# Splitting the odd stage's weights on GpSimd in whole instructions of 1,024 columns instead of four of 256

## The chip, the core and the metric

The kernel runs on one core of a Trainium2 chip. Its engines are TensorE (PE in the rows, with its weight loads as PEld), VectorE (DVE), ScalarE (ACT), GpSimd (POOL) and SyncE (SP), which issues most of the DMAs. The metric is the device time of one execution in microseconds; three runs of the kernel before gave 3427.5, 3423.56 and 3424.99 us, median 3424.99. Numbers such as 1036.13 are times from the span's start in the profiled execution.

## The reference

Two small transformer-like blocks run one after the other on 512 latent tokens and 256 context tokens of width 1,024. The first block has an even layer (a chunk MLP beside differential attention), then an odd layer (windowed attention with a sink), each followed by a SwiGLU network; the second block has a gated recurrent layer and a latent attention layer. The change lies in the projections of the odd layer, `h @ w_qkv`:

```python
q, k, v = jnp.split(h @ w_qkv, [C_Q_WIDTH, C_Q_WIDTH + C_KV_WIDTH], axis=-1)
q = apply_rope(q.reshape(b, s_len, C_HEADS, HEAD_DIM), cos, sin)...
k = apply_rope(k.reshape(b, s_len, C_KV_HEADS, HEAD_DIM), cos, sin)
kc, vc = jnp.split(hc @ w_qkv[:, C_Q_WIDTH:], 2, axis=-1)
...
s = einsum(q, k) * ATTN_SCALE                     # a band of up to 384 keys, and 256 context keys
p = softmax(concatenate(scores + [s_sink]))       # per 128 queries and head
out = einsum(p, v)
```

The weights `w_qkv` are 12 tiles of 128x1024 in float32: 8 for the queries, 2 for the keys, 2 for the values.

## The kernel before, in words

**Products in three parts.** A product of float32 matrices is made of three float32r matmuls: high weights by high tokens, high weights by low tokens, low weights by high tokens. So each weight tile must be split into a high part (rounded to float32r) and a low part (the tile minus its high part). In the odd stage GpSimd does that, in `split` (lines 661 to 670). Line 665 multiplies a piece of the tile in `ringA` by one and writes it rounded to `ringB_r`; a drain follows (line 666); line 668 subtracts and writes the low part into `ringA_r`, in place; then the semaphore `splitA` rises. The argument `n` says how many columns one instruction takes.

**The ring.** `ringA` has four slots. SP loads a tile (line 509) when `readA` says that TensorE has done with what was in the slot, and GpSimd splits it when `landedA` says that it has landed. All twelve tiles of the stage go through this in order, tile by tile (`split_A`, lines 672 to 677). The stages before and after use the same function: `ffn_out0` splits in whole tiles, `odd_out` in quarters, `ffn_in1` and `ffn_out1` whole.

**The odd stage.** First VectorE and ScalarE make the normalised tokens: line 2665 scales them, ScalarE's line 1972 rounds the high part, line 2587 makes the low part `a_r`; before that, line 2649 makes the coefficients. TensorE then computes tiles 0, 1 and 2 together, chunk by chunk (line 812), and tile 3 in two halves (line 1340). VectorE turns the first queries and keys by the rotary tables (lines 3049, 3050 and 3052, each with 512 columns, the two sets one after the other). The attention follows in 32 units, U = 0 to 31. For each, TensorE makes scores (1421 to 1430), VectorE the row maxima (3059 to 3064), ScalarE the exponentials (2237), VectorE the sums and the normalised p (3070 to 3074), TensorE the transposes (1444), ScalarE copies (2245), and TensorE the product with the values (1455). Between these TensorE puts pieces of the projections of tiles 4 to 11 (line 1340). Scores of the first unit wait for both rotary steps; scores of a later unit wait for the exponentials of the one before. Each engine works through its instructions in the written order; semaphores alone join them.

**Which tiles when.** Tiles 4 to 7 are loaded as slots 0 to 3 come free, near the end of the products of tiles 0 to 3. Tiles 8 to 11 are loaded one at a time, each when TensorE has finished the projection of the tile four places before it.

Of the kernel before, what the change touches and what calls it, by code (L numbers as in the profile page):

```python
# [15 lines left out]
D = 1024  # L16
# [88 lines left out]
def build(nc, streamA, streamB, streamC, x_in, ctx2_in, smalls_in, consts_in, lvl_in, sgu_in, out):  # L105
    with ExitStack() as ctx:
# [5 lines left out]
        def sem(name):  # L112
            if name not in sems:
                sems[name] = ctx.enter_context(nc.semaphore(name))
            return sems[name]

        def both(name, shape):

            with nc.sbuf_tensor(name, shape, F32) as v:
                pass  # L120
            return v, sb(name + "_r", shape, F32R)
# [9 lines left out]
        ringA, ringA_r = both("ringA", [P, RA, D])  # L131
        ringB, ringB_r = both("ringB", [P, RB, D])
# [85 lines left out]
        def landedA_at(name, g, k):  # L218
            return 16 * ((START_A[name] + k) // RA + 1) + g * (16 * COUNT[name][1] // RA)
# [177 lines left out]
        def high_slot(name, s):  # L397

            return (s + 1) % RA if name == "mla_out" else s
# [259 lines left out]
        def _(pool):  # L659

            def split(ring, ring_r, slot, high_r, high_slot, done, n=D // 4):

                parts = [slice(at, at + n) for at in range(0, D, n)]
                for t in parts:
                    nc.gpsimd.tensor_tensor(high_r[:, high_slot, t], ring[:, slot, t], ones[:, 0:1].broadcast_to([P, n]), ALU.mult)  # L665
                pool.drain()  # L666
                for t in parts:
                    last = nc.gpsimd.tensor_tensor(ring_r[:, slot, t], ring[:, slot, t], high_r[:, high_slot, t].bitcast(F32),  # L668
                                                   ALU.subtract)
                last.then_inc(sem(done), 1)  # L670

            def split_A(name):
                with pool.Fori(0, COUNT[name][0]) as g:
                    for k in range(COUNT[name][1]):
                        s = k % RA
                        pool.wait_ge(landedA[s], landedA_at(name, g, k))
                        split(ringA, ringA_r, s, ringB_r, high_slot(name, s), "splitA", D // 4 if name in ("even_out", "odd") else D)

            def split_hg_out():

# [92 lines left out]
            split_B("even")  # L773
            pool.wait_ge(sem("ev_exp"), 48)
            split_A("even_out")
            wi_products()
            for g in range(COUNT["ffn_out0"][0]):
                for k in range(COUNT["ffn_out0"][1]):
                    pool.wait_ge(landedA[k % RA], landedA_at("ffn_out0", g, k))
                    if g == 0 and k < RA:  # L780
                        pool.wait_ge(sem("wi_read"), max(n for n in range(len(PRODUCTS)) if n % RB == k) + 1)
                    split(ringA, ringA_r, k % RA, ringB_r, k % RA, "splitA", D)
            split_A("odd")
            pool.wait_ge(sem("od_p"), 60)
            split_odd_out()
            split_A("ffn_in1")
            split_A("ffn_out1")
            pool.wait_ge(sem("hg_free"), HEADS + 1)
# [2815 lines left out]
```

## Time and profile before

| what | value |
|---|---|
| runs | 3427.5, 3423.56, 3424.99 us |
| profiled execution | 3423.45 us, its span 3421.7 us |
| TensorE busy | 3251.4 us (95%) |
| VectorE busy | 2040.7 us (60%) |
| ScalarE busy | 1259.1 us (37%) |
| GpSimd busy | 1117.8 us (33%), 909 instructions |
| GpSimd in the odd stage, line 665 | 48 instructions of 128x256, 29.7 us |
| GpSimd in the odd stage, line 668 | 48 instructions of 128x256, 37.7 us |

The span is what the profiler saw on the core; the execution's own time is 1.75 us longer. A busy engine is not the same as one that others wait for: the waits in square brackets behind a row say how long its engine had sat idle before it, and what ended that.

### The profile page before, as it was taken

To read this page: it belongs to the slowest core of one execution; us is meant where nothing else is said; L and a number is where in the kernel's file an instruction comes from. 1 tells how busy PE (TensorE), PEld (TensorE's weight loads), DVE (VectorE), ACT (ScalarE), POOL (GpSimd) and SP (SyncE) were. 2 spreads that over 40 slices of the span, in tenths; PEclk is the share of its full clock that TensorE was granted. 3 is DMA by queue.
4 is the path that set the end of the run, shared out by engine and by line. 5 is a ranking of instruction groups with operands and counts; after the bars stand their busy time and mean duration, and the time that the engine had idled before them with its cause. 6 is when DMAs were issued, how large, how long until landed. Compare 5 with 4: busy or idle time off the path is not lost.

```text
span 3421.7 us, 53881 instructions
## 1 busy us (share of the span) xinstructions
PE 3251.4 (95%) x21096; PEld 2864.3 (84%) x21096; DVE 2040.7 (60%) x3136; ACT 1259.1 (37%) x2098; POOL 1117.8 (33%) x909
## 2 busy tenths in 40 slices
PE   7998989999998988999999999999999998999998
PEld 5776889999986666777799999999999697788876
DVE  4455554445345654023758787887878764566667
ACT  3444253332224541101244334343443223455542
POOL 3341565556544136677800000000000161222225
PEclk9999999999999999999999999999999997999999
DMA  6222244434211124444321111111110321111112
GB/s 265 87 87 111 86 172 150 162 125 181 81 56 38 32 75 166 169 176 166 106 77 53 53 49 52 49 49 44 44 45 31 117 62 62 38 49 37 48 68 80
DMA packets 85626, 307.62 MB, mean 90 GB/s; under 512 B 8496, under 2 KB 10544, under 8 KB 84400
## 3 DMA queue, kind: packets, MB, share of 16 engines
q1 hardware_dynamic: 78688, 286.89, 25.1%
q10 hardware_dynamic: 6736, 17.83, 1.4%
q8 instruction: 153, 2.51, 0.3%
q14 instruction: 49, 0.40, 0.0%
HBM read 281.61 MB, written 23.07 MB: 89 GB/s over the span
## 4 chain that ended last, share of the span: by engine, by line
PE 71%; DVE 14%; DVEq 4%; issue 4%; POOL 3%; ACT 3%; POOLq 1%; DMA 1%; SPq 0%; ACTq 0%
PE ps L812 20%; PE ps L951 14%; PE ps L1107 9%; PE ps L1691 4%; PE ps L1729 2%; DVE arena L3136 2%; DVEq L3127 2%; DVE arena L3126 2%; DVE rstd L3142 2%; PE ps L927 2%; DVE arena L3132 1%; PE ps L1340 1%; POOL ringA_r L668 1%; DVE arena L3123 1%; POOLq L666 1%
## 5 line engine op out<-in xcount | busy, mean ns | idle before, releaser
L665 POOL TENSOR_TENSOR ringB_r<-ringA,consts 128x1024 fp32r<-128x1024 f32 (+1 forms) x226 | 318.5, 1423 | 1545.6 <-DVE arena L3211 1021.5
L812 PE MATMUL ps<-x_r,ringA_r 128*128 128x384 f32 (+1 forms) x1912 | 557.0, 356 | 8.7 <-DVE a_r L2587 5.3
L812 PE MATMUL ps<-x_r,ringB_r 128*128 128x384 f32 (+1 forms) x1912 | 543.2, 349 | 10.1 <-DVE a_r L2587 9.0
L668 POOL TENSOR_TENSOR ringA_r<-ringA,ringB_r 128x1024 fp32r<-128x1024 f32 (+1 forms) x226 | 392.9, 1753 | 21.3 <-issue 0.4
L812 PEld LDWEIGHTS ps<-x_r,ringB_r 128*128 128x128 f32 x1912 | 350.1, 189 | 34.0 <-POOL ringA_r L668 9.2
L812 PE MATMUL ps<-a_r,ringA_r 128*128 128x384 f32 x1472 | 375.3, 335 | 0.0
L812 PEld LDWEIGHTS ps<-x_r,ringA_r 128*128 128x128 f32 x1912 | 338.7, 189 | 35.8 <-issue 8.5
L951 PE MATMUL ps<-a_r,ringB_r 128*128 128x384 f32 (+1 forms) x1376 | 340.4, 357 | 20.5 <-DVE a_r L2699 11.6
L951 PEld LDWEIGHTS ps<-a_r,ringB_r 128*128 128x128 f32 x1376 | 251.1, 191 | 41.3 <-DVE a_r L2699 17.7
L2699 DVE TENSOR_TENSOR a_r<-arena,a_r 128x768 fp32r<-128x768 f32 (+1 forms) x120 | 176.0, 1504 | 169.7 <-ACT a_r L2133 169.4
L812 PEld LDWEIGHTS ps<-a_r,ringA_r 128*128 128x128 f32 x1472 | 266.7, 188 | 0.0
L951 PE MATMUL ps<-a_r,ringA_r 128*128 128x384 f32 (+1 forms) x688 | 205.5, 355 | 0.0
L1107 PE MATMUL ps<-arena_r,ringB_r 128*128 128x384 f32 x1008 | 189.7, 339 | 2.1 <-POOL ringB_r L744 1.4
L2133 ACT ACTIVATE a_r<-arena 128x768 fp32r<-128x768 f32 (+1 forms) x120 | 83.3, 733 | 278.4 <-PE ps L951 270.4
L1107 PEld LDWEIGHTS ps<-arena_r,ringB_r 128*128 128x128 f32 x1008 | 176.8, 190 | 2.8 <-POOL ringB_r L744 1.7
L812 PE MATMUL ps<-a_r,ringB_r 128*128 128x512 f32 (+1 forms) x440 | 164.2, 385 | 0.0
L716 POOL TENSOR_TENSOR x_r<-ringA,consts 128x256 fp32r<-128x256 f32 x64 | 37.2, 613 | 342.9 <-DVE arena_r L3284 283.9
L744 POOL TENSOR_TENSOR ringB_r<-ringB,ringB_r 128x512 fp32r<-128x512 f32 x84 | 110.0, 1321 | 117.0 <-DVE ringB L2784 82.8
L2910 DVE TENSOR_TENSOR arena<-arena,ps 128x512 f32<-128x512 f32 x22 | 15.1, 688 | 218.6 <-PE ps L812 207.1
L1691 PE MATMUL ps<-arena_r 128*128 128x256 f32 (+1 forms) x768 | 141.8, 310 | 2.3 <-DVE arena_r L3270 1.5
L2699 DVE TENSOR_TENSOR arena_r<-arena,arena_r 128x768 fp32r<-128x768 f32 (+1 forms) x64 | 110.5, 1765 | 49.7 <-ACT arena_r L2133 49.4
L1107 PE MATMUL ps<-x_r,ringB_r 128*128 128x384 f32 x504 | 139.9, 338 | 0.0
(427 smaller groups left out, 6747.2 us busy)
## 6 DMA issues: line engine op xcount, KB each, us to landing
ringA<-streamA SPq DMA_DIRECT2D x232, 512.0 KB, 3.6
arena<-streamC SPq DMA_DIRECT2D x140, 512.0 KB, 6.5
ringB<-streamB SPq DMA_DIRECT2D x100, 512.0 KB, 3.6
x_scratch<-x ACTq DMA_DIRECT2D x8, 1024.0 KB, 6.8
x<-x_in SPq DMA_DIRECT2D x2, 3072.0 KB, 11.1
hid_scratch<-arena SPq DMA_DIRECT2D x16, 384.0 KB, 3.9
arena<-hid_scratch SPq DMA_DIRECT2D x1, 6144.0 KB, 22.4
x<-x_scratch SPq DMA_DIRECT2D x3, 2048.0 KB, 11.0
```

Of the source, the lines that this page charges most:

```text
L665: nc.gpsimd.tensor_tensor(high_r[:, high_slot, t], ring[:, slot, t], ones[:, 0:1].broadcast_to([P, n]), ALU.mult)
L668: last = nc.gpsimd.tensor_tensor(ring_r[:, slot, t], ring[:, slot, t], high_r[:, high_slot, t].bitcast(F32), ALU.subtract)
L744: nc.gpsimd.tensor_tensor(low, weight_source(p, j), high.bitcast(F32), ALU.subtract).then_inc(sem("wi_low"), 1)
L812: mm = nc.tensor.matmul(ps[:, bank + half, 0:tn], wk, src[:, k, t], start=k == 0 and i == 0, stop=k == DC - 1 and i == 2)
L927: mm = nc.tensor.matmul(ps[32 * j:32 * j + 32, b, at:at + 256], spad[:, vec, 2 * t + k, :], ring[:, t, k, r * 256:(r + 1) * 256], start=t ...
L951: mm = nc.tensor.matmul(ps[:, 2 * n + half, 0:tn], w, src[:, t], start=k == 0 and i == 0, stop=k == nk - 1 and i == 2)
L1107: mm = nc.tensor.matmul(ps[:, bank, 0:HALF], wk[:, w], src, start=p in ("P1", "P2", "P5", "P3") and c == 0 and i == 0, stop=c == 3 and i = ...
L1691: mm = nc.tensor.matmul(out, w, src, start=start and i == 0, stop=stop and i == 2, skip_group_check=True)
L1729: mm = nc.tensor.matmul(ps[:, 7, :], w, src[:, k, 0:LAT], start=k == 0 and i == 0, stop=k == DC - 1 and i == 2)
L2133: nc.scalar.activation(out_ring(name, p, chunk.shape[-1])[0], chunk, ACT.Copy).then_inc(sem("out_high"), 1)
L2699: TT(low, chunk, high.bitcast(F32), ALU.subtract).then_inc(sem("out_low"), 1)
L3126: TT(halves(H["ql"][:, p, :], h), halves(B["q"], h), P_queries, ALU.mult).then_inc(sem("hg_lvl"), 1)
```

## The change

In the odd stage the last argument of `split` becomes `D` (1,024) instead of `D // 4` (256), so that a tile takes one instruction of line 665 and one of line 668 instead of four of each. The stage `even_out` keeps its quarters, and so does `odd_out`, which has its own loop. Nothing else is changed: not the order of tiles, the loads, nor what any engine waits for.

```diff
                     for k in range(COUNT[name][1]):
                         s = k % RA
                         pool.wait_ge(landedA[s], landedA_at(name, g, k))
-                        split(ringA, ringA_r, s, ringB_r, high_slot(name, s), "splitA", D // 4 if name in ("even_out", "odd") else D)
+                        split(ringA, ringA_r, s, ringB_r, high_slot(name, s), "splitA", D // 4 if name == "even_out" else D)
```

On GpSimd, from the last tiles of `ffn_out0` into the first three of the odd stage's twelve, there stands before (`ringA` is the tile that was loaded, `ringB_r` its high part, `ringA_r` its low part, `consts` holds the ones):

```order
143 L665 TENSOR_TENSOR ringB_r<-ringA,consts 128x1024
144 L668 TENSOR_TENSOR ringA_r<-ringA,ringB_r 128x1024
145 L673 UNCONDITIONAL_BRANCH
146 L665 TENSOR_TENSOR ringB_r<-ringA,consts 128x256 x4
147 L668 TENSOR_TENSOR ringA_r<-ringA,ringB_r 128x256 x4
148 L665 TENSOR_TENSOR ringB_r<-ringA,consts 128x256 x4
149 L668 TENSOR_TENSOR ringA_r<-ringA,ringB_r 128x256 x4
150 L665 TENSOR_TENSOR ringB_r<-ringA,consts 128x256 x4
151 L668 TENSOR_TENSOR ringA_r<-ringA,ringB_r 128x256 x4
```

And at the same place now:

```order
143 L665 TENSOR_TENSOR ringB_r<-ringA,consts 128x1024
144 L668 TENSOR_TENSOR ringA_r<-ringA,ringB_r 128x1024
145 L673 UNCONDITIONAL_BRANCH
146 L665 TENSOR_TENSOR ringB_r<-ringA,consts 128x1024
147 L668 TENSOR_TENSOR ringA_r<-ringA,ringB_r 128x1024
148 L665 TENSOR_TENSOR ringB_r<-ringA,consts 128x1024
149 L668 TENSOR_TENSOR ringA_r<-ringA,ringB_r 128x1024
150 L665 TENSOR_TENSOR ringB_r<-ringA,consts 128x1024
151 L668 TENSOR_TENSOR ringA_r<-ringA,ringB_r 128x1024
```

No instruction has moved. Each group of four has become one, so the stage has 24 of these instructions where it had 96. The order of every other engine is the same.

## Rows read from the trace of the kernel before

**Rows 1.** The page: the chain that ended last, by engine.

```profile
PE 71%; DVE 14%; DVEq 4%; issue 4%; POOL 3%; ACT 3%; POOLq 1%; DMA 1%; SPq 0%; ACTq 0%
```

**Rows 2.** Timeline of GpSimd, 964 to 988: start, duration, what, [idle before <-releaser].

```profile
964.95 1.89 POOL L665 TENSOR_TENSOR ringB_r<-ringA,consts 128x1024 fp32r<-128x1024 f32 x1 [4.51 <-DMA ringA<-streamA]
966.99 2.38 POOL L668 TENSOR_TENSOR ringA_r<-ringA,ringB_r 128x1024 fp32r<-128x1024 f32 x1
...
981.06 2.33 POOL L665 TENSOR_TENSOR ringB_r<-ringA,consts 128x256 fp32r<-128x256 f32 x4 [2.90 <-DMA ringA<-streamA]
983.53 2.82 POOL L668 TENSOR_TENSOR ringA_r<-ringA,ringB_r 128x256 fp32r<-128x256 f32 x4
```

**Rows 3.** Timeline of GpSimd, tiles 2 and 3 of the odd stage.

```profile
995.85 2.75 POOL L665 TENSOR_TENSOR ringB_r<-ringA,consts 128x256 fp32r<-128x256 f32 x4 [9.50 <-DMA ringA<-streamA]
...
1003.93 3.22 POOL L668 TENSOR_TENSOR ringA_r<-ringA,ringB_r 128x256 fp32r<-128x256 f32 x4
```

**Rows 4.** Timeline of VectorE, the low parts of the first normalised tokens.

```profile
1005.61 1.82 DVE L2587 SCALAR_TENSOR_TENSOR a_r<-a,mod,x_r 128x512 fp32r<-128x512 f32 x2 [0.20 <-ACT x_r L1972]
...
1008.41 1.14 DVE L2587 SCALAR_TENSOR_TENSOR a_r<-a,mod,x_r 128x512 fp32r<-128x512 f32 x2
```

**Rows 5.** Timeline of GpSimd, tiles 4 to 7.

```profile
1033.58 2.33 POOL L665 TENSOR_TENSOR ringB_r<-ringA,consts 128x256 fp32r<-128x256 f32 x4 [26.43 <-DMA ringA<-streamA]
1036.05 4.22 POOL L668 TENSOR_TENSOR ringA_r<-ringA,ringB_r 128x256 fp32r<-128x256 f32 x4
1040.23 2.77 POOL L665 TENSOR_TENSOR ringB_r<-ringA,consts 128x256 fp32r<-128x256 f32 x4
...
1053.90 2.81 POOL L668 TENSOR_TENSOR ringA_r<-ringA,ringB_r 128x256 fp32r<-128x256 f32 x4
```

**Rows 6.** Timeline of VectorE beside tiles 4 to 6.

```profile
1036.13 1.20 DVE L3050 TENSOR_TENSOR arena<-arena,consts 128x512 f32<-128x512 f32 x1
1037.41 1.07 DVE L3052 TENSOR_TENSOR arena<-arena 128x512 f32<-128x512 f32 x1
...
1039.01 0.68 DVE L3050 TENSOR_TENSOR arena<-arena,consts 128x512 f32<-128x512 f32 x1
1039.76 1.06 DVE L3052 TENSOR_TENSOR arena<-arena 128x512 f32<-128x512 f32 x1
1042.35 1.29 DVE L3059 TENSOR_REDUCE st<-ps 128x1 f32<-128x512 f32 x2 [1.53 <-PE ps L1430]
...
1043.96 0.61 DVE L3063 TENSOR_SCALAR st<-st 128x2 f32<-128x2 f32 x1
1044.48 0.15 DVE L3064 TENSOR_TENSOR st<-smalls,st 128x2 f32<-128x2 f32 x1
```

**Rows 7.** Timeline of TensorE, the first scores.

```profile
1040.96 0.70 PE L1421 MATMUL ps<-arena 64*128 64x256 f32 x4 [1.18 <-DVE arena L3052]
```

**Rows 8.** Timeline of GpSimd, whole instructions in ffn_in1 and ffn_out1.

```profile
1306.65 2.35 POOL L668 TENSOR_TENSOR ringA_r<-ringA,ringB_r 128x1024 fp32r<-128x1024 f32 x1
...
1591.95 2.34 POOL L665 TENSOR_TENSOR ringB_r<-ringA,consts 128x1024 fp32r<-128x1024 f32 x1
```

**Rows 9.** Timeline of VectorE beside these.

```profile
1307.12 1.90 DVE L2649 SCALAR_TENSOR_TENSOR coef<-mod,smalls 128x16 f32<-128x16 f32 x1
...
1586.53 13.40 DVE L2699 TENSOR_TENSOR a_r<-arena,a_r 128x512 fp32r<-128x512 f32 x6 [3.11 <-ACT a_r L2133]
```

**Rows 10.** Timeline of VectorE beside tile 8.

```profile
1064.96 1.01 DVE L3074 TENSOR_SCALAR arena<-arena,st 128x640 f32<-128x640 f32 x1
...
1067.74 0.73 DVE L3064 TENSOR_TENSOR st<-smalls,st 128x2 f32<-128x2 f32 x1
```

**Rows 11.** Windows: length, each engine's busy us, then granted clock, DMA share, GB/s.

```profile
1046.00:1051.00 5.00, 4.74 (x19) 2.98 (x19) 3.44 (x8) 0.80 (x3) 4.86 (x8) 0.50 0.00 0
...
1071.00:1076.00 5.00, 3.11 (x34) 2.04 (x30) 3.56 (x12) 2.19 (x6) 0.43 (x1) 1.00 0.00 0
...
1131.00:1136.00 5.00, 5.00 (x33) 3.84 (x32) 3.31 (x9) 1.52 (x5) 3.89 (x7) 1.00 0.06 21
```

## The prediction

> **What bounds the kernel now.** I read the page first: TensorE holds 71% of the chain that ended last, VectorE 14%, GpSimd 3% [rows 1]. GpSimd is no bound over the whole, so the question is what its instructions do to others in the odd stage. Next came GpSimd's timeline there, then VectorE's in the same stretches, and last the TensorE windows.
>
> The reader is to see three things. GpSimd waits for the DMA of its tile, not the other way: 9.50 us before tile 2, 26.43 us before tile 4 [rows 3, 5]. Tiles 4 to 7 then form one burst without an idle bracket, from 1033.58 to 1056.71 [rows 5]. And in that burst VectorE does the rotary products and the first maxima, with TensorE waiting: the first scores at 1040.96 waited 1.18 us for VectorE's L3052 [rows 7]. The weights are not late there; VectorE is.
>
> **The change: what it saves.** A tile cost 2.33 us for L665 and 2.82 for L668 where VectorE kept away, and 5.29 us from first start to last end (981.06 to 986.35). Whole instructions of the stage before cost 1.89 and 2.38, and 4.42 us in all (964.95 to 969.37) [rows 2]. So 0.87 us less a tile, 12 tiles: 10.4 us of GpSimd time, over 72 fewer instructions. It is worth something only where a reader waits. TensorE starts on tiles 0 to 2 when the first normalised tokens are there, at 1007.43 (1005.61 + 1.82), and tile 3's L668 is already at work from 1003.93 [rows 3, 4]. Tile 4's split ended at 1040.27 [rows 5]; in TensorE's order its products stand behind the scores of two units, and the second scores wait for exponentials later than 1044.6 [rows 6]. I cost the saving itself at nothing; what hides it is that earlier work of TensorE.
>
> The shorter splits do one thing for the norm. Tile 2's split starts at 995.85 [rows 3]. With the old collision kept (2.75 against 2.33, so 0.42), whole it is 2.31 + 0.14 + 2.38, to 1000.7; tile 3 then runs to about 1005.1, where before its L668 ran 1003.93 to 1007.15. VectorE's first two L2587, which TensorE waits for, start at 1005.61 and took 1.82 us; the next two took 1.14 [rows 3, 4]. Tile 3 would be out of their way: **-0.7 us**.
>
> **The change: what it costs.** The trace shows what a VectorE instruction does that meets a whole GpSimd instruction. At 1306.65 GpSimd's L668 ran 2.35 us, to 1309.00; VectorE's L2649, all of 128x16, began at 1307.12 and took 1.90, to 1309.02 [rows 8, 9]. It waited for the end of the whole instruction. In a burst like ours both alternate: six L2699 took 13.40 us, 2.23 each, and GpSimd's L665 there 2.34, 0.45 over its 1.89 [rows 2, 8, 9]. So the one that waits gets its turn next, and VectorE gets one such operation per GpSimd instruction. (The Trainium skill, SBUF — State Buffer, "Who interferes with whom", says that whoever issues first has the shared port pair for the whole instruction, and that a tensor_tensor with two inputs in SBUF and a fast tensor_scalar contend while tensor_reduce does not; the trace agrees with the 1.90.) Which operations of ours are touched is seen from the stretched ones: L3050 1.20 and L3052 1.07 and 1.06 against 0.68 for the L3050 that met nothing, L3063 0.61 for two columns; the reductions L3059 from PSUM are not [rows 6]. With quarters such a wait ends after at most 0.8 us; whole it lasts up to 1.9 or 2.4.
>
> I walk the burst on the old clock, with 1.89 for L665, 2.35 for L668, and 0.55 for a 512-column VectorE operation once it has the turn. Tile 4: L665 1033.58 to 1035.47, L668 1035.61 to 1037.99. VectorE's first L3050 wants to start at 1036.13: it runs 1037.99 to 1038.55. Tile 5's L665 stood in line and takes 1038.55 to 1040.42; the first L3052 ends at 1040.97. L668 of tile 5 to 1043.3; second L3050 to 1043.85; L665 of tile 6 to 1045.7; second L3052 ends at 1046.25. Before it ended at 1040.82 [rows 6]: **+5.4 us** on the scores, which wait for nothing else. Scores and the reductions take as long as before (1.5 + 1.3 us and a little), so that L3061 wants its turn at 1049.1, while L665 of tile 7 holds to 1050.5. L3063 then waits for tile 7's L668, to 1053.0, and L3064 ends at 1053.3. Before, from the end of L3052 to the end of L3064 it was 1040.82 to 1044.63, 3.8 us [rows 6]; now 7.0: **+3.2 us**. The exponentials wait for it, and the second scores for them. GpSimd is then done, and what follows in VectorE is free. The bounds of these 8.6 us: below, if a waiting operation got in among the 1,024 columns, nothing is added and the stretches of the old rows go (0.52 + 0.38 + 0.37 + 0.44 = -1.7); above, TensorE's clock. It idles longer, and after a window like this the granted clock was 0.50, the 1.2 GHz level [rows 11]. I take no more of it than before, since the slow stretch moves along with the idle one; it may cost 1.5 us more.
>
> Queued behind each waiting VectorE instruction is its whole stream of maxima and normalisations; ScalarE's exponentials and TensorE's scores and transposes wait for these, and SP's next loads for TensorE's release of a slot. All of it moves along, so the later splits meet the same VectorE work as before.
>
> Tiles 8 to 11 are split singly, at 1065.00 and three times more. Tile 8: L3074 began at 1064.96 and took 1.01, about half of it waiting, so GpSimd had the turn [rows 10]; whole, L3074 ends at 1067.4 (+1.4). L668 then runs 1067.4 to 1069.75; L3061 wants 1068.7 and waits; L3064 ends at 1070.3 instead of 1068.47 (+1.8). The rotary step behind it is then free of GpSimd and regains some; the p that the transposes wait for comes +1.0 later, and TensorE idles there already (busy 3.11 of 5.00 us) [rows 11]. Tile 9 falls on the same work, with L3061 at the very edge: +0.8. Tiles 10 and 11 fall where TensorE is busy with projection pieces (5.00 of 5.00 us at tile 11 [rows 11]): 0.1 and 0, and at most 1.0 and 1.7 if that cover fails. Together **+1.9 us**, between -1.8 (no such lock; the waiting inside the 1.01 and the 0.73 of rows 10, about 1.0 a tile in tiles 8 and 9, less what lay off the path) and +6.3.
>
> Tiles 0 and 1 meet only VectorE work that reads PSUM. The sum: -0.7 + 5.4 + 3.2 + 1.9 = **+9.8 us**. The profiled execution took 3423.45 us (span 3421.7), so 3433.3; the median shown, 3424.99, lies 1.5 above it, and by that it would be 3434.8. I say **3434 us**.
>
> **The rivals.** (a) *The waits are there but partly absorbed.* If VectorE slips into the 0.14 us between L665 and L668 or at a changed phase, or part of the wait lies beside TensorE's leftover pieces, half of the 8.6 goes and the single tiles cost 0 to 1: +3 to +5, 3427 to 3429. For it: in the old rows some operations (the second L3050, 0.68) met no wait at all. Against it: the burst has GpSimd always standing in line, the scores already waited 1.18 us, and the sum of the waits is fixed by when the burst ends, near 1053.
>
> (b) *No lock: the port is shared in small pieces, so longer instructions stretch VectorE no more than quarters did, or less.* Then -0.7 - 1.7 - 1.8 = -4.2, 3419 against the profiled execution, 3421 against the median: within what can't be told from no change. Against it stands the 1.90 us for 16 columns.
>
> (c) *The other side: GpSimd's time is the bound.* If TensorE or the port waited for every split, all 10.4 us would come back: 3413 to 3415, faster. It decides from the point where a tile's first product starts within 0.9 us of the end of its split. For it: TensorE's start after 1007.43 lies right behind L668's end at 1007.15. Against it: that L668 is tile 3's, whose products come after all of tiles 0 to 2; everywhere else POOL is the one that waits for the DMA. [...]
>
> (d) *More than I walked.* The clock and the cover at tiles 10 and 11 fail: +9.8 + 1.5 + 2.6, 3437 to 3439.
>
> **How the numbers follow.** Less than about 0.2% of 3425, 6.9 us, is what a measurement of this kernel can't tell from no change. My forecast with (d): 0.79, nearly all above 3431.9. (a): 0.14. (b): 0.05. (c): 0.02. The range leaves out (b), (c) and a little above: 3427 to 3440. Faster 0.02, same 0.20, slower 0.78.
>
> **What would show it.** In the profile after: L665 and L668 of the stage as 12 rows each of 128x1024, tiles 4 to 7 done about 3 us earlier after their start; the first scores (L1421) waiting some 6 us for L3052 instead of 1.18; L3050, L3052, L3061 or L3063 of 1.5 to 2.6 us in the burst, one per GpSimd instruction; the start of L812 0.7 us earlier; the first split of odd_out some 10 us later. I am wrong if the L3052 before the first scores ends before 1043, if no VectorE operation of the stage exceeds 1.3 us (b), or if the delay at 1053 has vanished by the stage's end (a).

## The result, and the profile after

| | before | after |
|---|---|---|
| median, us (range, runs) | 3425.34 (3423.56 to 3428.97, 8) | 3435.81 (3432.02 to 3441.31, 8) |
| ratio after / before | | 1.0031, 95% interval 1.0022 to 1.0041 |
| profiled execution, its span | 3423.45, 3421.7 | 3436.25, 3434.5 |
| VectorE busy | 2040.7 | 2051.9 |
| GpSimd busy, instructions | 1117.8, 909 | 1106.7, 837 |

The kernel became slower by 10.5 us (7.5 to 14 by the interval); 3434 was predicted, in 3427 to 3440. GpSimd saved 11.1 us and VectorE's busy time grew by 11.2 with the same instructions: one that waits for GpSimd counts as busy (L3063, 2.36 us below, took 0.61 before). The shares of the chain that ended last [rows 1] moved little, TensorE's from 71% to 68% and GpSimd's from 3% to 4%:

```profile
PE 68%; DVE 14%; issue 4%; DVEq 4%; POOL 4%; ACT 3%; POOLq 2%; DMA 1%; SPq 0%; ACTq 0%
```

GpSimd's timeline after, tiles 4 to 7 (start, duration, instruction), answers to [rows 5]:

```profile
1035.98 1.89 POOL L665 TENSOR_TENSOR ringB_r<-ringA,consts 128x1024 fp32r<-128x1024 f32 x1 [28.21 <-DMA ringA<-streamA]
1038.02 2.40 POOL L668 TENSOR_TENSOR ringA_r<-ringA,ringB_r 128x1024 fp32r<-128x1024 f32 x1
1040.37 2.34 POOL L665 TENSOR_TENSOR ringB_r<-ringA,consts 128x1024 fp32r<-128x1024 f32 x1
1042.86 2.60 POOL L668 TENSOR_TENSOR ringA_r<-ringA,ringB_r 128x1024 fp32r<-128x1024 f32 x1
1045.43 2.34 POOL L665 TENSOR_TENSOR ringB_r<-ringA,consts 128x1024 fp32r<-128x1024 f32 x1
...
1050.47 1.89 POOL L665 TENSOR_TENSOR ringB_r<-ringA,consts 128x1024 fp32r<-128x1024 f32 x1
1052.51 2.34 POOL L668 TENSOR_TENSOR ringA_r<-ringA,ringB_r 128x1024 fp32r<-128x1024 f32 x1
```

And VectorE's beside it, to set against [rows 6]:

```profile
1037.93 0.69 DVE L3049 TENSOR_TENSOR arena<-ps,consts 128x512 f32<-128x512 f32 x1 [14.06 <-PE ps L1325]
1038.53 2.43 DVE L3050 TENSOR_TENSOR arena<-arena,consts 128x512 f32<-128x512 f32 x1
1041.04 2.23 DVE L3052 TENSOR_TENSOR arena<-arena 128x512 f32<-128x512 f32 x1
...
1043.79 2.23 DVE L3050 TENSOR_TENSOR arena<-arena,consts 128x512 f32<-128x512 f32 x1
1046.09 2.22 DVE L3052 TENSOR_TENSOR arena<-arena 128x512 f32<-128x512 f32 x1
1050.90 1.29 DVE L3059 TENSOR_REDUCE st<-ps 128x1 f32<-128x512 f32 x2 [2.59 <-PE ps L1430]
1052.27 0.16 DVE L3061 SCALAR_TENSOR_TENSOR st<-st,smalls 128x2 f32<-128x2 f32 x1
1052.51 2.36 DVE L3063 TENSOR_SCALAR st<-st 128x2 f32<-128x2 f32 x1
1054.78 0.15 DVE L3064 TENSOR_TENSOR st<-smalls,st 128x2 f32<-128x2 f32 x1
```

Read the two side by side. The burst lasts 18.87 us (1035.98 to 1054.85) where it lasted 23.13. But L3050 starts at 1038.53 inside GpSimd's L668, which ends at 1040.42, and ends at 1040.96, about 0.55 us later. Each of the four rotary operations with both inputs in SBUF ends about 0.55 us after the end of a GpSimd instruction: one gets through per instruction of 1,024 columns. Two columns wait as long as 512: L3063 takes 2.36 us and ends with the burst. L3049 (0.69) and L3059 (1.29), which read PSUM, wait for nothing.

TensorE's first scores, to set against [rows 7]:

```profile
1048.46 1.23 PE L1421 MATMUL ps<-arena 64*128 64x256 f32 x4 [6.28 <-DVE arena L3052]
```

They waited 6.28 us instead of 1.18, and then took 1.23 us instead of 0.70. The second is the clock. Windows of the kernel after (length; PE, PEld, DVE, ACT, POOL busy; then granted clock, DMA share, GB/s), and of the kernel before at the same times:

```profile
1045.00:1050.00 5.00, 1.54 (x8) 1.27 (x8) 3.23 (x2) 0.00 (x0) 4.86 (x3) 0.50 0.00 0
1050.00:1055.00 5.00, 0.86 (x6) 0.13 (x2) 3.87 (x5) 0.03 (x1) 4.70 (x3) 0.50 0.00 0
1055.00:1060.00 5.00, 3.44 (x15) 2.20 (x16) 1.89 (x7) 1.50 (x5) 0.00 (x0) 0.50 0.00 0
```

```profile
1045.00:1050.00 5.00, 3.74 (x17) 2.50 (x18) 2.88 (x7) 1.20 (x4) 4.86 (x8) 0.53 0.00 0
1050.00:1055.00 5.00, 5.00 (x19) 3.38 (x19) 1.98 (x5) 0.98 (x2) 4.86 (x9) 0.78 0.01 3
1055.00:1060.00 5.00, 5.00 (x43) 3.62 (x42) 3.51 (x9) 2.24 (x8) 1.71 (x3) 1.00 0.00 0
```

In both kernels TensorE idles and then runs at the 1.2 GHz level. After, it idles longer, and windows of 1 us from 1036 to 1096 give 17 us at the low level instead of 7 (a window counts in full at a granted clock of 0.50, not at all at 1.00, and in proportion between).

**The stage in parts.** To compare kernels whose starts differ by some us, I cut each trace at events of the stage:

| part, us | before | after | difference |
|---|---|---|---|
| last residual step of ffn_out0 (VectorE L2717) to TensorE's first L812 | 13.48 | 12.80 | -0.68 |
| to the first L3049 | 27.95 | 28.26 | +0.31 |
| rotary step, to the end of the second L3052 | 5.29 | 10.38 | +5.09 |
| first maxima, to the end of the first L3064 | 3.81 | 6.62 | +2.81 |
| to the first split of odd_out | 195.51 | 195.86 | +0.35 |
| whole stage | 246.04 | 253.92 | +7.9 |

"Stage" means this whole below. What lies before it (994.1 and 996.87 from the span's start) and behind it (2181.56 and 2183.71) is the same code, and over the other eight kernels of this case it varies from 992.0 to 996.2 and from 2179.8 to 2187.7. So 4.9 us of the 12.8 between the two spans lie outside the stage; I take them for scatter, though the change's own 996.87 is the latest start of all ten. Inside the stage, parts in which two kernels do the same work agree closely: the rotary step took 4.02 or 4.03 us in the three kernels with a wait and in the one without reading, and 10.35 and 10.38 in the two with a whole burst. A profile thus tells the stage more sharply than the total, though each stage below is of one profile.

### The profile page after: what moved, and what is told of

It is laid out like the page before. It is cut to its first block, busy times and chain, and to the rows that moved or that the text cites. A ratio compares the mean times of both kernels' runs of the same rounds, so it can differ in the third digit from the quotient of the medians.

```text
span 3434.5 us, 53809 instructions
## 1 busy us (share of the span) xinstructions
PE 3251.8 (95%) x21096; PEld 2864.8 (83%) x21096; DVE 2051.9 (60%) x3136; ACT 1259.2 (37%) x2098; POOL 1106.7 (32%) x837
## 4 chain that ended last, share of the span: by engine, by line
PE 68%; DVE 14%; issue 4%; DVEq 4%; POOL 4%; ACT 3%; POOLq 2%; DMA 1%; SPq 0%; ACTq 0%
PE ps L812 19%; PE ps L951 13%; PE ps L1107 9%; PE ps L1691 4%; PE ps L1729 2%; DVE arena L3136 2%; POOL ringA_r L668 2%; DVEq L3127 2%; POOLq L666 2%; DVE arena L3126 2%; DVE rstd L3142 2%; DVE arena L3132 1%; PE ps L1340 1%; DVE arena L3123 1%; PE ps L927 1%
## 5 line engine op out<-in xcount | busy, mean ns | idle before, releaser
L665 POOL TENSOR_TENSOR ringB_r<-ringA,consts 128x1024 fp32r<-128x1024 f32 (+1 forms) x190 | 312.8, 1655 | 1566.7 <-DVE arena L3211 1021.7
L812 PE MATMUL ps<-x_r,ringA_r 128*128 128x384 f32 (+1 forms) x1912 | 558.0, 357 | 11.1 <-DVE a_r L2587 4.7
L812 PE MATMUL ps<-x_r,ringB_r 128*128 128x384 f32 (+1 forms) x1912 | 544.8, 350 | 10.5 <-DVE a_r L2587 8.4
L668 POOL TENSOR_TENSOR ringA_r<-ringA,ringB_r 128x1024 fp32r<-128x1024 f32 (+1 forms) x190 | 386.8, 2045 | 21.4 <-issue 0.4
L812 PEld LDWEIGHTS ps<-x_r,ringB_r 128*128 128x128 f32 x1912 | 351.0, 189 | 34.8 <-issue 15.6
L812 PE MATMUL ps<-a_r,ringA_r 128*128 128x384 f32 x1472 | 376.0, 336 | 0.0
L812 PEld LDWEIGHTS ps<-x_r,ringA_r 128*128 128x128 f32 x1912 | 339.7, 189 | 38.2 <-issue 7.9
L812 PEld LDWEIGHTS ps<-a_r,ringA_r 128*128 128x128 f32 x1472 | 267.3, 189 | 0.0
L812 PE MATMUL ps<-a_r,ringB_r 128*128 128x512 f32 (+1 forms) x440 | 164.8, 386 | 0.0
## 6 DMA issues: line engine op xcount, KB each, us to landing
x<-x_scratch SPq DMA_DIRECT2D x3, 2048.0 KB, 10.7
```

Of the source, the lines that this page charges most:

```text
L812: mm = nc.tensor.matmul(ps[:, bank + half, 0:tn], wk, src[:, k, t], start=k == 0 and i == 0, stop=k == DC - 1 and i == 2)
```

## The experiments

All keep the loads, the order and every other engine's program unless said. Inserted lines shift the line numbers: by 1 in burst_whole, burst_quarters, halves and eighths, by 3 in the two with a wait, in staged by 4 for the rows shown of VectorE, by 5 in no_read; L3053 of halves is thus L3052 here.

| kernel | rotary step | first maxima | stage | median, us | ratio to before, 95% |
|---|---|---|---|---|---|
| before | 5.29 | 3.81 | 246.0 | 3425.34 | |
| after | 10.38 | 6.62 | 253.9 | 3435.81 | 1.0022 to 1.0041 |
| burst whole | 10.35 | 6.59 | 255.7 | 3434.73 | 1.0019 to 1.0043 |
| burst in quarters | 5.20 | 3.82 | 246.4 | 3425.60 | 0.9991 to 1.0009 |
| halves | 6.73 | 5.78 | 248.9 | 3427.01 | 0.9999 to 1.0017 |
| eighths | 4.25 | 3.76 | 244.0 | 3423.18 | 0.9992 to 1.0010 |
| wait, whole | 4.02 | 3.39 | 251.1 | 3431.42 | 1.0009 to 1.0027 |
| wait, quarters | 4.03 | 3.39 | 250.8 | 3431.14 | 1.0012 to 1.0031 |
| staged | 4.03 | 3.38 | 245.5 | 3426.21 | 0.9993 to 1.0011 |
| no reading | 4.02 | 3.40 | 241.8 | 3420.06 | 0.9978 to 0.9997 |

The ratios of the experiments are to other runs of the kernel before: 3425.17 (28 runs) for burst whole, burst in quarters, halves and wait whole, and 3424.88 (33 runs) for the other four.

### Which tiles cost: burst whole, burst in quarters

```diff
-  ... D // 4 if name in ("even_out", "odd") else D)
+  n = (D if 4 <= k < 8 else D // 4) if name == "odd" else ...      # burst whole
+  n = (D // 4 if 4 <= k < 8 else D) if name == "odd" else ...      # burst in quarters
```

> Only tiles 4 to 7 are split whole, the other eight of the odd stage in quarters. I measure the stage from the start of ffn_out0's last residual step (L2717) to the first split of odd_out: that is 246.0 us before (994.10 to 1240.14) and 253.9 after (996.87 to 1250.79). Theory 1 (VectorE's rotary step and first maxima wait for whole GpSimd instructions of the burst): the whole cost without the norm's gain, stage 254 to 255, time +8 to +9 against before. Rival 2 (a whole instruction costs about the same wherever it lies, so 4 of 12 tiles carry a third): stage 249, +3. Rival 3 (the extra time lies outside the stage, in how the program is laid out or fetched): stage near 246 to 247, time unlike that.

> The complement: tiles 4 to 7 in quarters, the other eight whole. Theory 1: the norm's -0.7 and some +0.8 at tiles 8 and 9 cancel, stage 246 to 246.5, time within 1 us of before. Rival 2: two thirds of the cost, stage 251, +5. Rival 3: time +2 to +3 or more with the stage near 246.

VectorE's end of the rotary step with only the burst whole, and then with only the burst in quarters:

```profile
1045.68 2.22 DVE L3053 TENSOR_TENSOR arena<-arena 128x512 f32<-128x512 f32 x1
...
1052.18 2.31 DVE L3065 TENSOR_TENSOR st<-smalls,st 128x2 f32<-128x2 f32 x1
```

```profile
1041.36 1.06 DVE L3053 TENSOR_TENSOR arena<-arena 128x512 f32<-128x512 f32 x1
```

Four tiles alone bring the whole loss, and eight whole tiles without them cost nothing that can be measured in the total: in their stage 0.4 us is won before the first L3049 and 0.8 lost behind the first maxima. The rivals "a cost in every tile" and "a cost outside the stage" fall. Burst whole missed its expectation by 0.7 us, upwards. That it comes out 1.75 us above the change itself is, by an estimate, mostly clock: with TensorE's busy time in each microsecond times (1 less the granted clock), summed from 1036 to 1096, as an estimate of what the low level cost, it has 5.3 us, the change 3.8, before 3.0.

### How the cost grows with the length: halves, eighths

```diff
+  n = D // 2 if name == "odd" else ...      # halves
+  n = D // 8 if name == "odd" else ...      # eighths
```

> All twelve tiles in two instructions of 512 columns. Theory 1: each of the five waiting operations in the burst waits up to 1.0 or 1.2 us instead of 2.4, so about a third of the cost remains: stage 248 to 249.5, +2 to +3.5. Rival 2 gives the same here. A rival by which only GpSimd's total time counted would put it between before and after in the other sense: less GpSimd time than quarters, so stage below 246.

> All twelve tiles in eight instructions of 128 columns. Theory 1 (VectorE waits for the rest of one GpSimd instruction): waits of at most 0.4 us; rotary step 4.6 to 5.0 instead of 5.3 (quarters), 6.7 (halves), 10.4 (whole); stage 245 to 246.3 though GpSimd needs more time per tile (some 6 us instead of 5.3). A theory by which GpSimd's total time holding the port counts would make it slower than quarters: stage 247 or more.

VectorE with halves, then GpSimd and VectorE with eighths:

```profile
1035.49 1.53 DVE L3051 TENSOR_TENSOR arena<-arena,consts 128x512 f32<-128x512 f32 x1
1037.10 1.63 DVE L3053 TENSOR_TENSOR arena<-arena 128x512 f32<-128x512 f32 x1
...
1044.20 1.29 DVE L3060 TENSOR_REDUCE st<-ps 128x1 f32<-128x512 f32 x2 [2.59 <-PE ps L1431]
```

```profile
1034.58 3.39 POOL L665 TENSOR_TENSOR ringB_r<-ringA,consts 128x128 fp32r<-128x128 f32 x8 [23.18 <-DMA ringA<-streamA]
1038.11 4.52 POOL L668 TENSOR_TENSOR ringA_r<-ringA,ringB_r 128x128 fp32r<-128x128 f32 x8
```

```profile
1039.88 0.79 DVE L3053 TENSOR_TENSOR arena<-arena 128x512 f32<-128x512 f32 x1
```

The stage follows the length: 244.0, 246.0, 248.9 and 253.9 us for 128, 256, 512 and 1,024 columns. With eighths GpSimd needs 8.05 us for tile 4 (1034.58 to 1042.63), almost twice the 4.44 of the change, and the stage is 9.9 us shorter. So what VectorE pays for is the length of the one instruction it meets, not the time that GpSimd spends on a tile. Halves landed on their expectation in the stage, and in the total a little below it (+1.8 us against +2 to +3.5, and not clear of noise); eighths came out about 1 us better than mine. In the total, eighths can't be told from before. Part of the growth is clock here too: halves had 14 us at the low level, before 7, eighths 3 (by the estimate above 4.2, 3.0 and 1.7 us lost), and the 2.59 before L3060 against 1.53 in the old rows is the scores at the low level.

### How much contention the kernel before already pays: no reading

Tiles 4 to 11 get two memsets instead of the two passes over the loaded tile, so the projections of these tiles are left out of the result.

```diff
+  if name == "odd" and k >= RA:
+      nc.gpsimd.memset(ringB_r[:, s, :].bitcast(F32), 0.0)
+      pool.drain()
+      nc.gpsimd.memset(ringA_r[:, s, :].bitcast(F32), 0.0).then_inc(sem("splitA"), 1)
+      continue
```

> Tiles 4 to 11 aren't split: GpSimd writes zeros over both parts with one whole memset each, which reads nothing from SBUF (so the products of these tiles come out zero; tiles 0 to 3 in quarters as before). It shows what the contention costs in all, and which of VectorE's operations meet a GpSimd instruction that only writes. Theory 1: the rotary step's tensor_tensors with two SBUF inputs wait for nothing: rotary step 4.0 to 4.2, first maxima 3.3 to 3.6, stage 241 to 243. If a write alone holds the VectorE operations off as a reading instruction does, L3050 and L3052 are stretched by up to a memset's length and the step takes over 5.

GpSimd's timeline of this kernel, then VectorE's beside it:

```profile
1037.37 0.95 POOL L678 MEMSET ringB_r<- 128x1024 f32 x1
1038.44 0.95 POOL L680 MEMSET ringA_r<- 128x1024 f32 x1
...
1045.68 0.95 POOL L680 MEMSET ringA_r<- 128x1024 f32 x1
```

```profile
1037.92 0.68 DVE L3055 TENSOR_TENSOR arena<-arena,consts 128x512 f32<-128x512 f32 x1
1038.68 0.69 DVE L3057 TENSOR_TENSOR arena<-arena 128x512 f32<-128x512 f32 x1
...
1046.14 0.77 DVE L3079 TENSOR_SCALAR arena<-arena,st 128x512 f32<-128x512 f32 x1
...
1047.28 0.49 DVE L3079 TENSOR_SCALAR arena<-arena,st 128x512 f32<-128x512 f32 x1
```

The stage is 241.8 us, 4.3 below before: that is about all that shorter or better placed splits of tiles 4 to 11 could still bring here. It also tells what collides. L3055 and L3057, with both inputs in SBUF, run their 0.68 and 0.69 us over a GpSimd instruction that only writes; the normalising L3079 does meet the memset at 1045.68 and takes 0.77 instead of 0.49. By the Trainium skill, SBUF — State Buffer, "Who interferes with whom", an operation with two inputs in SBUF contends only with a GpSimd instruction that reads there, while a fast tensor_scalar contends with any; both rows agree.

### Moving the burst: wait whole, wait in quarters, staged

The splits of the burst are held until VectorE has finished the first maxima (semaphore `od_mx`), so that the rotary step and these maxima meet nothing.

```diff
+  if name == "odd" and k == RA:
+      pool.wait_ge(sem("od_mx"), 1)
+  n = D if name == "odd" else ...                                  # wait, whole
+  n = (D // 4 if 4 <= k < 8 else D) if name == "odd" else ...      # wait, quarters
```

Staged: tiles 0 to 3 whole; tile 4's high part whole at once, then the wait, then its low part and tiles 5 to 11 in quarters.

```diff
-  for t in parts:
+  for t in [slice(0, D)] if held else parts:
       nc.gpsimd.tensor_tensor(high_r[:, high_slot, t], ...)
   pool.drain()
+  if held:
+      pool.wait_ge(sem("od_mx"), 1)
...
+  n = (D if k < RA else D // 4) if name == "odd" else ...
+  split(..., n, name == "odd" and k == RA)
```

> All twelve tiles whole as in the changed kernel, but GpSimd waits before tile 4 until VectorE has the maxima of unit 0 (semaphore od_mx at 1), so the burst starts some 10 us later and misses the rotary step. Theory 1: the rotary step takes 4.1 to 4.3 us instead of 10.4, the first maxima 3.3, and the whole burst then falls on normalisations with some slack: stage 244.5 to 247, time -1 to +2 against before. Rival 2: no better than after, stage 252 to 254. If tiles 5 or 6 come late TensorE waits for GpSimd at L1340, which the waits would show.

> Tiles 0 to 3 whole; of tile 4 the high part in one whole instruction at once, before VectorE's first two-input operation, then a wait for VectorE's first maxima (od_mx at 1), then its low part and tiles 5 to 11 in quarters. Theory 1: norm 12.8 to TensorE's start instead of 13.5, rotary step 4.0 instead of 5.3, first maxima 3.4 instead of 3.8, and some 1 us lost again where the quarters now meet normalisations: stage 244.5 to 245.5 against 246.0 before, time -1.5 to 0, too little to tell by time alone. If a wait just moves the burst's whole cost along (what the kernel with the wait and whole instructions suggests, 251.1), the stage is 247 or more.

> Like the kernel that waits for the first maxima before tile 4, but tiles 4 to 7 in quarters (the other eight whole). Whole instructions there gave stage 251.1, with 202.6 us from the first maxima to the end instead of 195.5. Theory 1: rotary step 4.0, maxima 3.4, and behind them 1 to 3 us lost (quarters on normalisations, and tile 6 ready late for its product): stage 244.5 to 247. Rival (it is the late burst and not the length of its instructions that costs in the waiting kernel): stage 250 or more.

All three clear the two parts as expected (4.0 and 3.4 us). With whole instructions the loss comes back a little later. VectorE's timeline of wait whole, and a TensorE row beside it:

```profile
1042.90 2.44 DVE L3077 TENSOR_SCALAR arena<-arena,st 128x512 f32<-128x512 f32 x1
...
1051.79 2.39 DVE L3067 TENSOR_TENSOR st<-smalls,st 128x2 f32<-128x2 f32 x1
...
1056.34 2.50 DVE L3077 TENSOR_SCALAR arena<-arena,st 128x640 f32<-128x640 f32 x1
...
1067.10 2.30 DVE L3073 TENSOR_TENSOR st<-st 128x1 f32<-128x1 f32 x1
```

```profile
1058.90 0.76 PE L1447 MATMUL ps<-consts,arena 128*128 128x128 f32 x5 [1.21 <-DVE arena L3077]
```

My expectation for it missed by at least 4 us: I had taken the normalisations of the first units to be covered by TensorE's projection pieces, and the transposes wait for them. Such waits of TensorE for L3077 add up to 3.9 us between 1040 and 1071 (0.97, 1.21, 0.28 and 1.46).

The wait in quarters missed by nearly as much (3.8 us), and for another reason. By its number the rival of its expectation (the late burst costs, whatever its length: 250 or more) came true. Staged speaks against that rival: its burst starts as late, also in quarters, and its stage is 245.5. The two kernels differ in tile 4's high part, made early in staged, and in tiles 8 to 11, whole here. The first shows in one row: TensorE waited 1.81 us for the split of tile 6. Staged waited 1.60 for exponentials soon after, and at about 1064, counted from the start of the stage, this kernel is only 0.4 us behind it. Then tile 8, whole, stands right behind the burst. The VectorE and TensorE rows of this kernel, its windows, and those of staged:

```profile
1066.45 1.18 DVE L3064 SCALAR_TENSOR_TENSOR st<-st,smalls 128x2 f32<-128x2 f32 x1
...
1067.78 2.33 DVE L3067 TENSOR_TENSOR st<-smalls,st 128x2 f32<-128x2 f32 x1
```

```profile
1060.19 0.35 PE L1343 MATMUL ps<-x_r,ringB_r 128*128 128x256 f32 x1 [1.81 <-POOL ringA_r L668]
...
1071.84 0.78 PE L1424 MATMUL ps<-arena 64*128 64x256 f32 x4 [2.60 <-ACT arena L2240]
```

```profile
1070.00:1075.00 5.00, 2.82 (x14) 1.79 (x14) 4.61 (x12) 2.29 (x8) 0.10 (x1) 0.73 0.00 0
1075.00:1080.00 5.00, 3.88 (x24) 2.89 (x26) 2.04 (x10) 2.59 (x8) 0.00 (x0) 0.50 0.00 0
```

```profile
1070.00:1075.00 5.00, 3.26 (x32) 2.09 (x26) 4.23 (x13) 2.25 (x8) 0.72 (x1) 1.00 0.00 0
1075.00:1080.00 5.00, 4.66 (x40) 3.53 (x41) 3.28 (x10) 2.10 (x6) 0.00 (x0) 1.00 0.00 0
```

One whole tile delays L3067 by 2.2 us, TensorE waits 2.60, and the granted clock then falls to 0.50, where in staged it stays at 1.00. The estimate of the low level is 6.1 us here and 1.7 in staged: 4.4 of the 5.4 us between their stages. That the extra idle time brought the clock down is read from two traces, and was not tested by itself.

Staged met its expectation, with a stage 0.6 us under before, and no difference in the total. Of all these kernels only the one that leaves the projections out was faster than the one before, beyond its interval.

## Why the prediction was right, step by step

- **The saving, costed at nothing.** Right. GpSimd's burst was 4.3 us shorter, and nobody had waited for it; rival (c) needed the opposite. Burst in quarters keeps the saving in eight tiles and gains nothing: 246.4 against 246.0 us.
- **The norm, -0.7.** Measured -0.68. Tile 3's L668 was done by 1007.77 (below), before VectorE's first L2587 began. That began 11.51 us after the stage's start in both kernels (1005.61 less 994.10, 1008.38 less 996.87), and took 1.15 us where the old one took 1.82 [rows 4]: the whole gain is this. I did not ask how much of it lasts: at the first L3049 0.37 of it is left (+0.31 in the part behind), and the other four kernels with tiles 2 and 3 whole agree, with 41.06 to 41.08 us up to there against 41.43 before and 41.06 in the change.

```profile
1005.42 2.35 POOL L668 TENSOR_TENSOR ringA_r<-ringA,ringB_r 128x1024 fp32r<-128x1024 f32 x1
```

```profile
1008.38 1.15 DVE L2587 SCALAR_TENSOR_TENSOR a_r<-a,mod,x_r 128x512 fp32r<-128x512 f32 x2 [0.20 <-ACT x_r L1972]
```

- **The rotary step, +5.4.** Measured +5.09, by the mechanism walked: one operation per GpSimd instruction. Eighths, halves and no reading hold it up from both sides. Rival (b) falls with them, and rival (a), which had half of the waits absorbed, with this term and the stage.
- **The first maxima, +3.2.** Measured +2.81, but made otherwise. From the start of L3059 to the end of L3064 it is 2.28 us before and 4.03 after, so the lock took 1.75; the other 1.06 is the scores at the low clock (2.59 against 1.53 from L3052 to L3059). I had put the clock at zero and two waits for two GpSimd instructions. Because the scores were slow, L3061 came just as tile 7's L665 ended (0.16 us), and only L3063 waited. (In burst whole it is the next one, L3064, and the part is as long, 6.59.) Two errors, 1.06 us of clock left out and about 1.4 of lock too much (3.2 less 1.75), nearly cancelled: that this term fits is luck.
- **Between the maxima and tile 8** I had nothing; it is -0.35, read on TensorE: its second scores started 10.30 us later than before (1056.56 less 1046.26), its scores at tile 8 9.95 (1074.34 less 1064.39). The quarters went on to 1056.71 beside the second unit, and the whole burst ends with the first maxima. I read this as what paid for the longer low stretch; no run separates the two.
- **The single tiles, +1.9.** Mis-sized: +0.35 at tile 8, +0.4 at tile 9, nothing at 10 and 11, together about 0.7 (TensorE's lag went from 9.95 to 10.29 and 10.7, and stayed there). VectorE's rows at tiles 8, 9 and 10, against [rows 10]:

```profile
1074.78 0.55 DVE L3074 TENSOR_SCALAR arena<-arena,st 128x640 f32<-128x640 f32 x1
...
1077.33 2.31 DVE L3063 TENSOR_SCALAR st<-st 128x2 f32<-128x2 f32 x1
...
1104.28 2.36 DVE L3064 TENSOR_TENSOR st<-smalls,st 128x2 f32<-128x2 f32 x1
...
1128.78 2.20 DVE L3074 TENSOR_SCALAR arena<-arena,st 128x640 f32<-128x640 f32 x1
...
1132.24 0.98 DVE L3061 SCALAR_TENSOR_TENSOR st<-st,smalls 128x2 f32<-128x2 f32 x1
```

  I had two waits at tile 8, L3074 for L665 and L3061 for L668. In the old rows L3074 and L665 began within 0.04 us of each other (1064.96 and 1065.00), and L3074 took 1.01. Now L665 came at 1074.99, 0.21 us behind L3074, which took its plain 0.55; L665 waited instead (2.09 against 1.89), then lay beside the reduction L3059 that reads PSUM, and only L3063 waited. So VectorE lost 1.4 us up to the end of L3064 (a lag of 9.83, then 11.23), not 1.8, and won 0.94 of it back in the next L3052 and L3070, which in the old kernel had waited for the last quarters (1.06 and 0.68 us, now 0.69 and 0.15); at tile 9 it won back as much. "All of it moves along, so the later splits meet the same VectorE work as before" was the sentence that failed: they meet the same work, but a shift of 0.2 us decides who waits.
- **The sum.** +9.8 predicted, +7.9 in the stage of one pair of profiles, +10.5 (7.5 to 14) between the medians. The stage's value lies inside the interval. That 3434 comes within 1.8 us of the median is partly luck, since the stage is 1.9 us under my sum and 2.6 lie outside it. Whether the other 2.6 us are noise or a real cost elsewhere stays open; for burst whole the medians (3434.73 less 3425.17) and the stages (255.7 less 246.0) both differ by 9.6, so nothing there asks for a further cause. Of rival (d) the clock came, in part, and the failing cover at tiles 10 and 11 did not.

## What to carry to other kernels

In these traces a GpSimd instruction that reads SBUF held off VectorE's operations with two inputs in SBUF, and its tensor_scalar, until it ended (an operation then took up to 2.50 us at 1,024 columns). Where they meet, cut it by what a short VectorE operation on the critical path can afford to wait, not by GpSimd's own efficiency. Here 128 to 256 columns cost up to 3.6 us more GpSimd time a tile and 8 to 10 us less in the stage. Where GpSimd waits for its data anyway, a saving on it is worth nothing and only its side effects count; and moving its work in time helps only if the place it moves to has been walked with the same care.

## What the runs showed of the hardware that was not expected

- The lock seems to feed the clock; this is read from the traces and was not tested by itself. In the change TensorE's first scores waited 6.28 us for VectorE, and 17 us of the stage then ran at the 1.2 GHz level against 7 before and 3 with eighths. TensorE's waits in the rows don't show this part; the durations of its matmuls do (L1421 1.23 against 0.70 us).
- The size of the waiting operation hardly matters: 128x1 (2.30 us, L3073 in wait whole), 128x2 (2.36) and 128x512 (2.43) took about the same. Tiny operations on statistics held the exponentials.
- A memset of 128x1024 by GpSimd took 0.95 us, half of the cheapest pass that reads (1.89), and let two-input operations of VectorE run unstretched beside it.
- Of an instruction cut in four, the three more cost 0.44 us (2.33 against 1.89), about 0.15 us each.
